# Attention with turned scores in rounded products, two heads' P V in one run of the queue, residual in DRAM

## The reference

```
y = concat([ya, yb, yc, yd]) * silu(gate)        # gla, fox, mla, rg-lru
x = x + y @ w_out
```

```
s = q @ k.T * dk ** -0.5      (fox: + cum[query] - cum[key], a log-forget bias)
o = softmax(where(query >= key, s, -inf)) @ v
```

## Time and profile before

| | |
|---|---|
| runs | 3224.7, 3226.34, 3227.0 us (median 3226.34) |
| profiled execution, first to last instruction | 3222.3 us |
| the same against the median of the runs | 4.0 us less; no other time of the profiled execution is given |
| TensorE busy | 2601.3 us, 81% |
| VectorE, ScalarE, GpSimd busy | 42%, 27%, 15% |
| mean granted clock of TensorE | 0.904 of full speed |
| moved by DMA | 78.65 MB, mean 24 GB/s |

### The profile page before, as it was taken

One profiled execution on the slowest core, in us unless ns is written; L12 is line 12 of the kernel. 1 busy time (PEld: TensorE's weight loads), 2 busy tenths in 40 slices (PEclk: granted clock), 3 DMA queues, 4 the chain that ended last, 5 costly groups with the idle time before them and its releaser, 6 DMA issues. The chain is left out here.

```text
span 3222.3 us, 36887 instructions
## 1 busy us (share of the span) xinstructions
PE 2601.3 (81%) x14416; PEld 2124.9 (66%) x14416; DVE 1357.5 (42%) x2296; ACT 867.1 (27%) x1389; POOL 468.7 (15%) x308
## 2 busy tenths in 40 slices
PE   4976678998987898985868776889989878889766
PEld 3855568787766666773657555777877757677545
DVE  3119931522532545515231397225235336364153
ACT  3023310322311424305131233113123124342041
POOL 1115521010020000110111254210100200001111
PEclk9988989999988999998978888889999889999888
DMA  3000010000010000001010000100000100000102
GB/s 114 14 29 1 1 53 15 14 27 27 1 35 25 14 9 14 14 27 30 27 61 14 29 1 3 51 15 14 27 27 2 34 25 14 9 14 14 43 13 79
DMA packets 74534, 78.65 MB, mean 24 GB/s; under 512 B 16080, under 2 KB 63344, under 8 KB 74352
## 3 DMA queue, kind: packets, MB, share of 16 engines
q1 hardware_dynamic: 74352, 76.19, 7.5%
HBM read 71.99 MB, written 4.19 MB: 24 GB/s over the span
## 5 line engine op out<-in xcount | busy, mean ns | idle before, releaser
L892 PE MATMUL psum<-gla_ql,gla_kl 128*128 128x256 f32 x448 | 143.8, 476 | 102.6 <-DVE gla_ql L687 102.5
L892 PEld LDWEIGHTS psum<-gla_ql,gla_kl 128*128 128x128 f32 x448 | 104.4, 243 | 146.5 <-DVE gla_A L759 107.8
L484 DVE TENSOR_TENSOR x_res<-x_res,psum 128x512 f32<-128x512 f32 x128 | 86.0, 685 | 194.0 <-PE psum L503 193.8
L1106 DVE TENSOR_REDUCE fox_nmax<-psum 128x1 f32<-128x128 f32 (+7 forms) x128 | 97.0, 758 | 137.1 <-PE psum L1039 136.4
L1106 DVE TENSOR_REDUCE mla_nmax<-psum 128x1 f32<-128x128 f32 (+7 forms) x128 | 97.0, 758 | 136.6 <-PE psum L1039 135.8
L1125 ACT ACTIVATE mla_q<-psum,mla_nmax 128x128 f32<-128x128 f32 (+7 forms) x128 | 94.8, 741 | 205.6 <-DVE mla_nmax L1106 205.6
L1125 ACT ACTIVATE fox_qa<-psum,fox_nmax 128x128 f32<-128x128 f32 (+7 forms) x128 | 94.8, 741 | 205.6 <-DVE fox_nmax L1106 205.6
L1036 PE MATMUL psum<-fox_kT,fox_qT 66*128 66x512 f32 (+3 forms) x384 | 149.8, 500 | 0.0
L1036 PE MATMUL psum<-mla_kT,mla_qT 96*128 96x512 f32 (+3 forms) x384 | 149.8, 500 | 0.0
L1059 PE MATMUL psum<-fox_v,fox_ka 128*128 128x64 f32 x1152 | 142.7, 270 | 0.0
L1059 PE MATMUL psum<-mla_v,mla_k 128*128 128x64 f32 x1152 | 142.7, 270 | 0.0
(11 more groups left out here) (369 smaller groups left out, 5611.9 us busy)
## 6 DMA issues: line engine op xcount, KB each, us to landing
w_next<-in_w_in_dram SPq DMA_DIRECT2D x26, 1024.0 KB, 5.2
w_next<-in_w_out_dram SPq DMA_DIRECT2D x8, 1024.0 KB, 5.1
fox_w_raw<-in_w_in_dram SPq DMA_DIRECT2D x6, 1024.0 KB, 7.2
x_res<-in_x_dram SPq DMA_DIRECT2D x1, 4096.0 KB, 12.6
gla_w_raw<-in_w_in_dram SPq DMA_DIRECT2D x4, 1024.0 KB, 6.9
out_dram<-x_res SPq DMA_DIRECT2D x1, 4096.0 KB, 11.7
gla_w_raw<-in_w_in_dram SPq DMA_DIRECT2D x2, 1088.0 KB, 5.2
fox_w_raw<-in_w_in_dram SPq DMA_DIRECT2D x2, 1056.0 KB, 9.6
```

The costliest lines, as they stand in the source:

```text
L484: dve.tensor_tensor(at, at, k.psum[:, u % 8, :], ALU.add).then_inc(added, 1)
L892: last = pe.matmul(k.psum[:, n % NB, g * HH * HALF:(g + 1) * HH * HALF], kl[:, m % RING, g, :], ql[:, m % RING, g, :, :] .rearrange("p h t ...
L1106: dve.tensor_reduce(nmax[:, u:u + 1], score_ap(u), AX_X, ALU.max, negate=True)\
```

## The change

**Attention.** `turn_block` is gone. A new class, `Attention`, holds one half's attention in one block. It works in *items*: a pair of heads p (2) and a chunk c of 512 queries (2). An item has units (key block kb, head a): 8 for c = 0, 16 for c = 1. A unit covers 128 keys on partitions and up to 512 queries as columns. All 48 units of a call have 24 x 512, 8 x 384, 8 x 256 and 8 x 128 columns. The parts:

- q and k are transposed in groups of four (`turn`); ScalarE writes the rounded high part, VectorE the rest. The groups of the first pair stand at the call's start, those of the second beside item 1.
- The maxima come from scores in query order, one rounded product each (`score`), VectorE's `tensor_reduce` over a ring of two banks, a transpose of each column of negated maxima (`turn_max`), and ScalarE's copy into row 0 of `q_hi`; row 0 of k holds ones. So the scores come out of the product with the maximum subtracted.
- The scores with keys on partitions: three rounded products (`turned_scores`) and a mask; ScalarE's exponential into one of six slots.
- `pv`: v [128 keys, 64] is stationary and P (fp32, up to 512 queries) moves. Head a of the pair writes partitions 64a to 64a + 63 of one bank; the two heads' products stand next to each other in the list.
- GpSimd adds the P tiles up (`add`); a product of ones with the sum (`row_sums`) gives the row sums on all 64 partitions of a head. ScalarE inverts by Ln and Exp, VectorE refines, GpSimd multiplies the gate by it, VectorE multiplies with the result. No transpose of the result is left.

**Residual.** `x_res` is gone. The setup copies x from DRAM to the output in DRAM; `norm_block` loads it from there; `out_block` loads and stores tiles of 256 KB through a ring of six and waits for all stores at its end; `store_block` is gone.

**Layouts.** q and k carry a further element in front (row 0) and are ordered head by head; the forget bias of the query is left out, since the maximum subtracted takes it with it; gains are set to one first and the gains' DMA waits for that.

```diff
@@ norm_block
+                sp.dma_start(x[:, :, :], k.out[0].rearrange("(t p) n -> p t n", p=P)).then_inc(x_landed, 16)
                 sp.dma_start(gain[:, :], bcast_rows(d["norm_g"][layer], P)).then_inc(loaded, 16)
...
+                act.wait_ge(x_landed, 16)
@@ out_block
+        xt = k.sb(s, tag + "_xt", [P, XR, BANK])
...
+                for i in range(len(units) + 3):
+                    if i < len(units):
+                        if i >= XR:
+                            sp.wait_ge(x_stored[i % XR], 16 * (i // XR))
+                        sp.dma_start(xt[:, i % XR, :], rows(i)).then_inc(x_in[i % XR], 16)
+                    if i >= 3:
+                        u = i - 3
+                        sp.wait_ge(added, u + 1)
+                        sp.dma_start(rows(u), xt[:, u % XR, :]).then_inc(x_stored[u % XR], 16)
+                for i in range(XR):
+                    sp.wait_ge(x_stored[i], 16 * len(range(i, len(units), XR)))
...
                 for u, (n, t) in enumerate(units):
+                    dve.wait_ge(x_in[u % XR], 16 * (u // XR + 1))
                     dve.wait_ge(unit_done, u + 1)
-                    at = k.x[:, t, half(n)]
+                    at = xt[:, u % XR, :]
@@ class Attention
+    def scores_at(self, i, j):
+        if i + 1 == len(self.items):
+            return range(0)
+        if self.items[i][1] == 0:
+            return range(3 * j, min(3 * j + 3, 16)) if j < 6 else range(0)
+        return range(2 * (j - 8), 2 * (j - 8) + 2) if 8 <= j < 12 else range(0)
...
+        def score(i, n):
...
+            if u >= 2:
+                pe.wait_ge(self.max_done, u - 1)
+            out = k.psum[:, 2 + u % 2, :hi - lo]
+            diagonal = hi == (qt + 1) * P
+            last = pe.matmul(out, self.q_hi[:, h, qt * P:(qt + 1) * P], self.k_hi[:, h, lo:hi], start=True,
+                             stop=not diagonal)
...
+        def turned_scores(i, j):
...
+            if u >= 2:
+                pe.wait_ge(self.exp_done, u - 1)
+            out = k.psum[:, u % 2, lo:]
+            keys, queries = slice(kb * P, (kb + 1) * P), slice(c * BANK + lo, (c + 1) * BANK)
+            pe.matmul(out, self.k_hi[:, h, keys], self.q_hi[:, h, queries], start=True, stop=False)
+            pe.matmul(out, self.k_hi[:, h, keys], self.q_lo[:, h, queries], start=False, stop=False)
...
+            last = pe.matmul(out, self.k_lo[:, h, keys], self.q_hi[:, h, queries], start=False, stop=not diagonal)
...
+        def pv(i, j):
...
+            pe.wait_ge(self.exp_done, u + 1)
+            if j == 0 and i >= 2:
+                pe.wait_ge(self.y_done, i - 1)
+            pe.matmul(k.psum[a * HEAD:(a + 1) * HEAD, 4 + i % 2, lo:], self.v[:, kb, h * HEAD:(h + 1) * HEAD],
+                      self.p[u % self.PR][:, lo:], start=(kb == 0), stop=(kb == 4 * c + 3)).then_inc(self.pv_done, 1)
...
+        for i in range(len(self.items)):
+            for j in range(self.n_units(i)):
+                turned_scores(i, j)
+                late.append((i, j))
+                if j % 2 and len(late) > 2:
+                    pv(*late.pop(0))
+                    pv(*late.pop(0))
+                if self.pre_at(i, j) is not None:
+                    turn(*self.pre_at(i, j))
+                for n in self.scores_at(i, j):
+                    score(i + 1, n)
+                if self.m_at(i, j) is not None:
+                    turn_max(i + 1, self.m_at(i, j))
+                if i and j == 3:
+                    row_sums(i - 1)
...
+        def exponent(i, j):
...
+            if u >= self.PR:
+                act.wait_ge(self.pv_done, u - self.PR + 1)
+                act.wait_ge(self.acc_done, u - self.PR + 1)
+            act.activation(self.p[u % self.PR][:, lo:], k.psum[:, u % 2, lo:], ACT.Exp).then_inc(self.exp_done, 1)
+        def invert(i):
+            act.wait_ge(self.rs_done, i + 1)
...
+            act.activation(self.r0[:, :], k.psum[:, self.misc_bank("rs", i, 0), :], ACT.Ln).then_inc(self.ln_done, 1)
+            act.wait_ge(self.ln_done, i + 1)
+            act.activation(self.r0[:, :], self.r0[:, :], ACT.Exp, scale=-1.0).then_inc(self.r0_done, 1)
...
+    def gpsimd(self, pool):
+        def add(i, j):
...
+                pool.tensor_copy(acc, p).then_inc(self.acc_done, 1)
+            else:
+                pool.wait_ge(self.acc_done, u - 1)
+                pool.tensor_tensor(acc, acc, p, ALU.add).then_inc(self.acc_done, 1)
```

More of the change, by code:

```diff
@@ L440, in out_block @@
     nc = k.nc
+    XR = 6
     names = ["w_landed", "w_hi", "w_lo", "y_hi", "y_lo", "unit_done", "added"]
     w_landed, w_hi_ready, w_lo_ready, y_hi_ready, y_lo_ready, unit_done, added = map(k.sem, names)
+    x_names = [f"x_{what}{i}" for what in ("in", "stored") for i in range(XR)]
+    x_in, x_stored = [k.sem(n) for n in x_names[:XR]], [k.sem(n) for n in x_names[XR:]]
     NQ = D_MODEL // BANK
@@ L506, in _ @@
                                 last.then_inc(unit_done, 1)
-    k.clear(names, fetch_for=layer)
+    k.clear(names + x_names, fetch_for=layer)
 def gate_jobs(sg, mixer, chunks):
@@ L941, in gla_mix_block @@
     k.clear(names)
[L947 to L969, removed]
-                act.activation(qT[:, :, t * P:(t + 1) * P], src, ACT.Copy, scale=q_gain[:, 0:1]).then_inc(q_evac, 1)
-        @block.vector
-        def _(dve):
-            for t in range(TT):
-                dve.wait_ge(k_turned, t + 1)
-                src = k.psum[:width, RING + t % RING, :].rearrange("p (h n) -> p h n", h=HH)
-                dve.tensor_scalar(kT[:, :, t * P:(t + 1) * P], src, k_gain[:, 0:1], None, ALU.mult)\
-                   .then_inc(k_evac, 1)
-    k.clear(names)
@@ L1027, in _, with attention_block @@
+def attention_block(k, q_tok, k_tok, v, q_gain, k_gain, sg, width, tag, p_ring=None, acc=None):
+    with ExitStack() as s:
+        att = Attention(k, s, q_tok, k_tok, v, q_gain, k_gain, sg, width, tag, p_ring, acc)
+        with k.nc.Block() as block:
             @block.tensor
             def _(pe):
-                def score(u):
-                    qt, h = u // HH, u % HH
-                    if u >= 2:
-                        pe.wait_ge(probs, u - 1)
-                    out, n = score_ap(u), (qt + 1) * P
-                    for c0 in range(0, n, BANK):
-                        c1 = min(c0 + BANK, n)
-                        pe.matmul(out[:, c0:c1], qT[:, h, qt * P:(qt + 1) * P], kT[:, h, c0:c1], start=True,
-                                  stop=(c1 < n))
-                    pe.matmul(out[:, qt * P:n], k.ident_bf[:, :], k.mask_bf[:, :], start=False, stop=True)\
-                      .then_inc(scores, 1)
@@ L1064, in turn_y @@
-                def turn_y(qt):
-                    pe.wait_ge(normed, qt + 1)
-                    for i in range(HALF_W // P):
-                        last = pe.transpose(k.psum[:, B_O + qt % 2, HALF_W + i * P:HALF_W + (i + 1) * P],
-                                            on[:, i * P:(i + 1) * P], k.ident[:, :])
-                    last.then_inc(y_turned, 1)
-                warm_clock(k, pe, B_O + 1)
-                for u in range(U + 2):
-                    if u < U:
-                        score(u)
-                    if 1 <= u <= U:
-                        turn(u - 1)
-                    if u >= 2:
-                        pv(u - 2)
-                        if (u - 2) % HH == 1 and u - 2 > HH:
-                            turn_y((u - 2) // HH - 1)
@@ L1114, in _ @@
[L1114 to L1115 removed]
+                att.vector(dve)
             @block.scalar
             def _(act):
[L1119 to L1128 removed]
@@ L1129, in attention_block, with _ @@
-    k.clear(names)
+                att.scalar(act)
+            @block.gpsimd
+            def _(pool):
+                att.gpsimd(pool)
+    k.clear(att.names)
 def fox(k, layer):
```

461 lines of the change are left out of this document (302 added, 159 removed).

## The result

The changed kernel takes 3447.56 us (median of 4 runs, 3435.68 to 3452.52) where the kernel before takes 3225.52 beside it: a ratio of 1.0683, 95% interval 1.0663 to 1.0703. Slower, as forecast, but by 222 us and not by 59; the range (3205 to 3375) doesn't hold it. The profiled execution has a span of 3443.2.

The account below looks back on a forecast made before the run. TensorE's own queue was taken to bound attention's main loop. The span before, 3222.3, plus 12 for attention and 47 for the residual gave 3281; with the runs' median 4.0 above the span, 3285 us, range 3205 to 3375.

Parts of the forecast that it names:

- the residual: Norm, setup and output blocks: waits for DRAM loads and stores, less the dropped last store, +47 us (31 to 70).
- 1.5 us a call: Attention: a call takes 100.3 us against 98.85 before, +1.5, or +12 over eight calls.
- The clock: Half-idle start of each attention call: TensorE's clock falls to its lower level and returns, +2 us a call (0 to 5).
- P V at three quarters of the serial price: Attention's P V pairs: two heads' products partly overlap, three record times for four, 23.0 us a call; switches cost nothing.
- Rival (b): Attention: P V overlaps at half price, VectorE and GpSimd set the pace; 96 us a call, 3250 in all; 15%.
- rival (a): Attention: first cause, P V doesn't overlap; second, drains at switches cost 9.5 us a call; 3361 in all; 25%.
- Items 0, 1 and 2: Attention's main loop: 13.5, 25 and 15 us, from TensorE's work, VectorE's maxima, row sums and the division.
- The maxima pass: Attention: the additional query-order pass costs TensorE 8.6 us a call, plus masks, transposes of maxima and waits for VectorE.
- GpSimd: Attention's row-sum additions: 1.34 us per 512 columns, level with TensorE in item 3, below it in item 1.
- the chain at the end: Each attention call's end: row sums, ScalarE, VectorE and GpSimd passes, last product and waits after the last addition, 8 us.
- (c): Attention's main loop: half-price overlap, no waits left, GpSimd at its lower bound; 85 us a call, 3161 in all; 15%.
- (d): Attention's item 3: GpSimd's 512-column addition takes 1.60 us, +4 us a call, 3317 in all; 5%.

Follow-up runs that it names:

- the yardstick: The changed kernel with fox's q and k padded by zeros to 128 rows and 25 filler products at every call's start: 3327.35 us, ratio 1.032.
- the experiments with 66, 97 and 128: The changed kernel with fox's score products feeding 66 rows (ring of P buffers moved), 97 or 128 (both zero-padded, ring moved): 3454.68, 3382.45 and 3365.05 us.
- the residual alone: The kernel before with only x_res replaced by the DRAM version of the norm and output blocks, attention as before: 3265.52 us, ratio 1.0129.

## Why the prediction was wrong

The sign was right; the size was not. Of the forecast's +59, 47 were the residual, which came near; that attention would lose rested on 1.5 us a call, less than its terms were off by, and this part of the sign is luck. 162 us are missing between the forecast's span (3281) and the measured one (3443.2): 118 are the lower clock in the calls; 64 are what the calls take over the forecast at nearly full clock (866 against 802); 7 came back by the residual, 7 because mla calls before took 100.7 and not the 98.85 that was taken for all eight, and 6 outside the calls. By its steps:

**The clock: +2 a call (0 to 5): this is the step that failed.** It was put into the start alone, with products at the lower level in items 1 or 3 named as what would make the forecast too low; it was items 0 and 2. With 128 rows and fillers the eight calls take 866 us, and the products of the change 984: 118 us, 15 a call (23 in fox, 6 in mla), is what the lower clock costs over that. The items of the first call beside those of the yardstick and the forecast:

```
                 forecast   128 rows + fillers   changed kernel
start             19.3            20.4                21.3
item 0            13.5            15.4                25.1
item 1            25.0            27.2                28.3
item 2            15.0            17.5                23.8
item 3 and end    27.5            27.3                27.3
```

In fox two items of four run at the lower level for most of their length, in the later fox calls part of item 1 as well (2354.95 to 2387.95, 33.0); in mla it is item 0 alone (20.5 us for 15.4). What the forecast took from before, that a busy queue holds the full clock, does not hold for this mix of products: the change thins it out in columns (P V with 64 of 128 columns of the array), in waits (the maxima), and in rows (66 in the rounded products). The rows are shown by the experiments with 66, 97 and 128; so is the start. What the waits and P V's half width do to the clock is only argued, and why the clock answers to rows at all is open.

**P V at three quarters of the serial price: wrong in both of its parts, which nearly cancel.** Two heads overlap wholly (half the price, 9.4 us a call less than taken), and a switch costs 0.26 per run of P V, not 0: 23 runs, 6.0 us. Rival (b)'s price was true, and so was rival (a)'s drain, at two thirds of the 9.5 it had.

**Items 0, 1 and 2: 60.0 at full clock against 53.5.** The maxima pass was priced at some 20 us a call by the forecast's terms (5.3 at the start, 6.0, 2.3 and 6.2 in items 0, 1 and 2) and costs 25.6; in these three items it is 19.1 against 14.5. Part of that is the transposes of the maxima, taken at 0.06 and measured at 0.109 each, 1.6 a call. The change spends on the maxima more than it saves on transposes (17.4). At nearly full clock it is still slower than the kernel before (3327 against 3224), and without the maxima it is faster (3122): they decide the sign. P V's two errors give -3. A further term is at the passages. In the yardstick's first call:

```profile
693.48 0.50 PE L1125 MATMUL psum<-fox_q_hi,fox_k_hi 128*128 128x512 f32 x1
693.81 0.39 PE L1126 MATMUL psum<-fox_q_lo,fox_k_hi 128*128 128x512 f32 x1
...
694.28 0.40 PE L1125 MATMUL psum<-fox_q_hi,fox_k_hi 128*128 128x512 f32 x1
694.52 0.40 PE L1126 MATMUL psum<-fox_q_lo,fox_k_hi 128*128 128x512 f32 x1
```

The first score product of the unit at 693.48 follows P V, and the next product comes 0.33 later; the one at 694.28 follows rounded products, and it is 0.24. So it goes through the call: of the 48 first score products 38 are late by 0.03 to 0.11, and all of these but one follow P V, row sums, a mask or transposes; the other 10 follow a rounded product. Behind transposes nothing is lost by it, since the product started early, 0.03 and not 0.11 after the last transpose. Behind P V and masks some 1.8 us a call are. What is left of the 6.5 was not parted.

**GpSimd: right.** A 512-column addition takes 1.28 (forecast 1.34), and it is level with TensorE in item 3 and ends 1.5 us late there (lines of the changed kernel):

```profile
L1303 POOL TENSOR_TENSOR fox_acc<-fox_acc,fox_p 128x512 f32<-128x512 f32 x64 | 80.7, 1276 | 38.3 <-ACT fox_p L1202 38.0
...
725.23 1.08 PE L1147 MATMUL psum<-fox_acc,fox_ones 128*64 128x512 f32 x4 [1.53 <-POOL fox_acc L1303]
726.35 0.60 ACT L1208 ACTIVATE fox_r<-psum 128x512 f32<-128x512 f32 x1 [3.13 <-PE psum L1147]
...
730.50 0.69 DVE L1269 TENSOR_TENSOR fox_gate<-psum,fox_gate 128x512 f32<-128x512 f32 x1 [1.44 <-POOL fox_gate L1309]
```

The same lines are the chain at the end: from P V's end (723.7) to 731.19 it is 7.5, forecast 8.

**The residual: +47 forecast, +40 measured.** By the trace of the residual alone: the wait before the first square 24.1 in two (forecast 25), the setup 2.3 later (20.95 against 18.68 for its sine; forecast 5), the last store's 13.2 saved; by subtraction that leaves 27 for eight output blocks, 3.4 each (3.5 and 2 for clearing).

```profile
norm_x<-out_dram SPq DMA_DIRECT2D x2, 4096.0 KB, 13.4
...
out_dram<-fox_xt SPq DMA_DIRECT2D x32, 256.0 KB, 3.4
```

**The rivals.** (c) is excluded at its place: at nearly full clock a call takes 108 and not 93. (a) came nearest by its number, still 87 us short, and by its second cause, not by its first: P V does overlap. The call of its first cause adds up to 109.1 with the items given there, and not to 109.8 or 110. (d) is out: an addition takes 1.28 and not 1.60.

## What to carry to other kernels

When a change swaps dense full-array products for a mix with fewer rows or columns, price it at both clock levels: here the same attention takes 984 us, or 866 with rows of zeros and 25 fillers a call added. The zeros, which make the contraction full, were worth 82 us alone and cost two memsets for each half and storage that was free. Two heads' products that write different halves of the partitions belong side by side, and in longer runs, since each run pays once. A separate pass for the maxima is not free because its products are cheap: TensorE's own share was 12.4 by the forecast's sum, and leaving it out, with nine fillers, gave 25.6.

## What the hardware showed that was not expected

The granted clock stays at 1.2 GHz through stretches in which TensorE is busy all the time (630 to 635 and 645 to 650, and without a break from 2350 to 2365; 0.50). It depends on how many rows the products feed, zeros or not: 0.69 to 0.76 with 66 rows, 0.86 with 97, 0.89 to 0.96 with 128, in the same fox calls. Changed with the rows were the place of a ring, which was shown to do nothing, and the width of the 64 transposes that bring q and k in, which was not tested apart. The kernel before fed 66 rows too, in fp32 products, and held 1.00, so it is not the rows by themselves.
